# A decoder layer in float32 pairs: weight lows of the first FFN piece on VectorE, and TensorE's loop over the FFN pieces written out

## The reference

```
xm = rmsnorm(h, p['norm_mlp_g'])
h = h + jnp.square(jax.nn.relu(xm @ p['w_up'])) @ p['w_down']     # w_up 2048 x 8192, w_down 8192 x 2048
y = rmsnorm_final(h)
```

## Time and profile before

| | |
|---|---|
| median of 3 runs | 2808.96 us (2808.72 to 2814.73) |
| the profiled execution | 2811.47 us, of which the span of its instructions is 2809.4 us |
| TensorE busy | 2740.9 us, 98% of the span; mean granted clock 0.989 |
| VectorE, ScalarE, GpSimd busy | 55%, 32%, 22% |
| the first FFN piece on TensorE | 1359.0 to 1568.9 us |
| pieces 1 to 7 | 1568.9 us to the final transposes, some 174 us each |

### The profile page before, as it was taken

The page is one execution under the profiler, slowest core; times in us unless marked ns, Lnnn a source line. Parts: engine busy times, 40 slices in busy tenths (PEclk is TensorE's granted clock), DMA queues, the critical chain, the costliest instruction groups (busy, mean ns, idle before and its releaser), DMA issues.

```text
span 2809.4 us, 51396 instructions
## 1 busy us (share of the span) xinstructions
PE 2740.9 (98%) x21572; PEld 2624.0 (93%) x21572; DVE 1536.6 (55%) x2077; ACT 911.6 (32%) x1187; POOL 627.6 (22%) x278
## 2 busy tenths in 40 slices
PE   9999999999999999899988999999999999999998
PEld 7999998777999888699988999999999999999998
DVE  4677836667222344422354665746557465574765
ACT  5221125445222211232232332514325143251442
POOL 2455434675444322244330000000000000000000
PEclk9999999999999999999999999999999999999999
DMA  6733445655432655543227455464554635546443
GB/s 191 144 101 100 105 127 158 180 166 161 159 94 83 195 195 195 173 128 112 91 60 209 116 163 156 116 187 121 156 155 122 185 110 163 148 124 184 110 139 110
DMA packets 543266, 399.71 MB, mean 142 GB/s; under 512 B 35145, under 2 KB 464047, under 8 KB 541615
## 3 DMA queue, kind: packets, MB, share of 16 engines
q1 hardware_dynamic: 471032, 294.02, 36.4%
q10 hardware_dynamic: 72027, 102.69, 12.2%
HBM read 343.10 MB, written 53.84 MB: 141 GB/s over the span
## 4 chain that ended last, share of the span: by engine, by line
PE 72%; issue 13%; POOL 7%; DVE 5%; ACT 1%; DMA 1%; SPq 0%; POOLq 0%; DVEq 0%; ACTq 0%
PE lin L2248 26%; PE lin L1643 21%; PE aux L2213 17%; POOL wlo L883 4%; PE lin L2213 3%; POOL wlo L925 3%; PE aux L1920 1%; PE aux L1965 1%; DVE turn L2300 1%; PE lin L1733 0%; DVE rot L2300 0%; PE aux L1911 0%; PE aux L1810 0%; PE aux L1806 0%; DVE mixl L2300 0%
## 5 line engine op out<-in xcount | busy, mean ns | idle before, releaser
L883 POOL TENSOR_TENSOR wlo<-raw,whi 128x1024 fp32r<-128x1024 f32 x188 | 461.5, 2458 | 716.2 <-ACT whi L965 522.0
L2248 PE MATMUL lin<-fh,whi 128*128 128x260 f32 x2048 | 578.7, 283 | 13.0 <-DVE part L3127 10.4
L2248 PE MATMUL lin<-fl,whi 128*128 128x260 f32 x2048 | 578.9, 283 | 0.0
L2248 PE MATMUL lin<-fh,wlo 128*128 128x260 f32 x2048 | 578.9, 283 | 0.0
L2248 PEld LDWEIGHTS lin<-fh,whi 128*128 128x128 f32 x2048 | 387.0, 189 | 13.4 <-DVE wlo L3018 10.6
L1475 ACT ACTIVATE whi<-raw 128x1024 fp32r<-128x1024 f32 x212 | 224.2, 1058 | 511.8 <-DVE hr L3131 401.0
L2248 PEld LDWEIGHTS lin<-fh,wlo 128*128 128x128 f32 x2048 | 387.5, 189 | 0.0
L2248 PEld LDWEIGHTS lin<-fl,whi 128*128 128x128 f32 x2048 | 386.7, 189 | 0.0
L3018 DVE TENSOR_TENSOR wlo<-raw,whi 128x1024 fp32r<-128x1024 f32 x238 | 290.3, 1220 | 29.3 <-ACT whi L1475 29.3
L965 ACT ACTIVATE whi<-raw 128x1024 fp32r<-128x1024 f32 x140 | 147.5, 1058 | 472.6 <-PE lin L1643 324.0
L3127 DVE TENSOR_TENSOR part<-lin,rB 128x520 f32<-128x520 f32 x128 | 89.5, 699 | 382.4 <-PE lin L2248 375.9
(11 more groups left out here) (483 smaller groups left out, 6703.5 us busy)
## 6 DMA issues: line engine op xcount, KB each, us to landing
raw<-in_w_up SPq DMA_DIRECT2D x128, 512.0 KB, 4.3
raw<-in_w_down SPq DMA_DIRECT2D x128, 512.0 KB, 4.4
hr<-hscr ACTq DMA_DIRECT2D x128, 260.0 KB, 3.3
raw<-in_w_in SPq DMA_DIRECT2D x60, 512.0 KB, 3.9
hscr<-hr ACTq DMA_DIRECT2D x112, 260.0 KB, 2.1
raw<-in_w_out SPq DMA_DIRECT2D x32, 512.0 KB, 3.9
raw<-in_w_q SPq DMA_DIRECT2D x32, 512.0 KB, 4.0
piece<-in_cache_mem_k SPq DMA_DIRECT2D x32, 512.0 KB, 6.0
```

The source lines that it names most:

```text
L883: pool.tensor_tensor(wlo[:, slot, :], raw[:, slot % 2, :], whi[:, slot, :].bitcast(F32), ALU.subtract).then_inc(s.w_lo, 1)
L2248: mm = pe.matmul(lin[:, 2 * i + f, 0:HALF], w, x[:, kk, HALF * f:HALF * f + HALF], start=(first and m == 0 and part == 0), stop=(last and ...
```

## The change

It has two parts.

1. In the first FFN piece GpSimd makes no lows from the second pair on; its loop ends one turn after `T_MLP` begins, and the two units of `w_down` go too. VectorE makes them (`lo_slot`, `lo_down`). On VectorE and ScalarE the work of a pair is no longer in blocks: the four weight units, the two tiles and the two sets of sums are interleaved (`up_tile`, `up_low`, `sums_of`, `sums_low`).
2. On TensorE `with pe.Fori(1, N_CHUNK) as c` becomes `for c in range(1, N_CHUNK)`: the seven pieces stand one after the other in its list, with constants in the waits.

```diff
-            with pool.Fori(T_O + 1, T_MLP + QUADS) as T:
+            with pool.Fori(T_O + 1, T_MLP + 1) as T:
                 lo_turn(T)
-            for n in range(2):
-                pool.wait_ge(s.w_hi, unit_of(0, n) + 1)
-                pool.tensor_tensor(wlo[:, n, :], RAW4[n], whi[:, n, :].bitcast(F32), ALU.subtract).then_inc(s.w_lo, 1)
...
             for p in range(QUADS):
-                if p < QUADS - 1:
-                    hi_turn(p + T_MLP + 1)
-                else:
-                    hi_down(0, 0)
-                    hi_down(0, 1)
-                up_pair(p)
+                last = p == QUADS - 1
+                hi_down(0, 0) if last else hi_slots(p + T_MLP + 1, (0,))
                 combined(2 * p)
+                hi_down(0, 1) if last else hi_slots(p + T_MLP + 1, (1,))
+                up_tile(p, 0)
                 combined(2 * p + 1)
+                if not last:
+                    hi_slots(p + T_MLP + 1, (2, 3))
+                up_tile(p, 1)
...
-            with pe.Fori(1, N_CHUNK) as c:
+            for c in range(1, N_CHUNK):
                 for u in range(QUADS):
                     quad(c, u)
...
+            def lo_slot(T, slot):
+
+                n = 4 * T + slot
+                if n == 4 * (T_MLP + 1):
+                    v.wait_ge(s.w_lo, n)
+                v.wait_ge(s.w_hi, n + 1)
+                v.tensor_tensor(wlo[:, slot, :], raw[:, slot % 2, :], whi[:, slot, :].bitcast(F32),
+                                ALU.subtract).then_inc(s.w_lo, 1)
...
             for p in range(QUADS):
-                up_pair(p)
+                last = p == QUADS - 1
+                lo_down(0, 0) if last else lo_slot(T_MLP + p + 1, 0)
+                sums_of(2 * p)
+                up_tile(p, 0)
+                sums_low(2 * p)
+                lo_down(0, 1) if last else lo_slot(T_MLP + p + 1, 1)
+                up_low(p, 0)
+                sums_of(2 * p + 1)
+                if not last:
+                    lo_slot(T_MLP + p + 1, 2)
+                sums_low(2 * p + 1)
+                up_tile(p, 1)
                 if p == 0:
                     inverse(6, D, 2)
-                combined(2 * p)
-                combined(2 * p + 1)
+                if not last:
+                    lo_slot(T_MLP + p + 1, 3)
+                up_low(p, 1)
```

More of the change, by code:

```diff
@@ L1580, in down, with up_tile @@
                     square_h(n) if end else store_h(c, n)
[L1582 to L1587, removed]
+            def up_tile(p, i):
+                act.wait_ge(s.tile_free, 2 * p + (O_MLP + i + 1))
+                act.activation(hsqF[:], upr[:], ACT.Square).then_inc(s.up_sq, 1)
+                act.wait_ge(s.up_sq, 4 * p + 2 * i + 2)
+                act.activation(fh[:, 2 * p + i, :], hsqF[:], ACT.Copy).then_inc(s.hid_hi, 1)
             def combined(k):
@@ L2219, in quad @@
                 Q = quad_of(c, q)
-                if not (isinstance(c, int) and c == 1 and q == 0):
+                if Q > 0:
                     pe.wait_ge(s.up_sq, act_n(Q - 1, 4))
@@ L2989, in _, with up_tile, up_low, sums_of @@
                 step.leave(7)
[L2990 to L3002, removed]
+            def lo_slot(T, slot):
[5 more added lines that the diff above has]
+                                ALU.subtract).then_inc(s.w_lo, 1)
+            def up_tile(p, i):
+                v.wait_ge(s.pe_unit, 4 * (T_MLP + p) + 2 * i + 2)
+                if p == 0 and i == 1:
+                    v.wait_ge(s.stat_mm, stat_n(6))
+                if p + i > 0:
+                    v.wait_ge(s.hid_lo, 2 * p + i)
+                v.tensor_scalar(halves(upr[:]), lin_tile(i), 0.0, None, ALU.max).then_inc(s.tile_free, 1)
+            def up_low(p, i):
+                v.wait_ge(s.hid_hi, 2 * p + i + 1)
+                v.tensor_tensor(fl[:, 2 * p + i, :], hsqF[:], fh[:, 2 * p + i, :].bitcast(F32),
+                                ALU.subtract).then_inc(s.hid_lo, 1)
+            def sums_of(k):
                 for j in range(2):
@@ L3009, in combined, with sums_low @@
                 tt(tsum[:, 3, :], tsum[:, 1, :], msum[:, 1, 0, :], ALU.subtract, s.t_dve)
-                v.wait_ge(s.up_sq, 4 * (k // 2) + 2 + k % 2 + 1)
+            def sums_low(k):
+                v.wait_ge(s.up_sq, 2 * k + 1)
                 tt(tl[:, :, k, :], tsum[:], th[:, :, k, :].bitcast(F32), ALU.subtract, s.t_dve)
@@ L3015, in lo_unit @@
                 v.wait_ge(s.w_hi, n + 1)
-                if n == unit_of(0, 2):
-                    v.wait_ge(s.w_lo, n)
                 v.tensor_tensor(wlo[:, slot, :], src, whi[:, slot, :].bitcast(F32), ALU.subtract).then_inc(s.w_lo, 1)
```

## The result

The changed kernel takes 2775.8 us (median of 4 runs, 2773.1 to 2778.8) against 2809.8 us before (2808.7 to 2814.7): ratio 0.9876, 95% interval 0.9859 to 0.9893, 34.0 us less. The forecast was 2775.0 us, 34.0 us less.

A forecast was written before the change was run, and what follows sets the result against it. TensorE, busy 98% of the span, bounds the kernel, through its waits and low clock. First piece 25.6 plus loop 8.4 gives 34.0 us off 2811.5; against the median before, 2775.0 us forecast, range 2770 to 2787.

The forecast's parts named there:

- The first piece, 25.6 us: Second pair to end of first FFN piece: 17.8 us idle plus low clock behind it, 25.6 us in all, would go.
- cause (a): First piece: next pair's roundings stand behind both `th`, GpSimd's lows come late; waits of 2.0, 2.8 and 2.6 us would go.
- ScalarE's late roundings: First piece: ScalarE rounds the next pair's first two units only behind both `th`; the two roundings last 1.99 us.
- Cause (b): End of first piece: loads for `down` wait for the last `tl`, making `part` late; TensorE's 10.4 us wait would go.
- E - 1.5: First piece's last pair: the last `tl` would end near 1.5 us before the last `w_up` unit ends (E).
- The cover of 0.7 us at E: First `down`: `part` done at E + 10.8, TensorE supplied to E + 11.5; in time by 0.7 us, the thinnest cover.
- `fl`: VectorE's subtraction in the first piece: 0.70 us each time instead of up to 1.81, moving nothing in the sum.
- The loop, 8.4 us: TensorE's pieces 1 to 7 written out: 13.5 us of return costs leave, 5.1 come back as boundary waits; net 8.4 us.
- the momentary low clock: At one of the loop's six returns the clock falls for a moment: 10.41 against 8.87 us for the same 72 matmuls.
- the prediction's lower bound of 6.9: Loop's gain is 6.9 us if the momentary low clock belongs to chance and comes elsewhere.
- The seven waits: Piece boundaries after the change: seven waits of about 0.6 us for VectorE's low replace the 10.4 us "issue" entry.
- stay near 159: TensorE's instruction queue: its packet count would stay near 159 with the loop written out.

The follow-up runs named there:

- woven_gpsimd: Changed kernel (woven order, loop written out) with the first piece's 14 lows left on GpSimd; 2777.8 us, ratio to before 0.9887.
- block_vector: Kernel before with the loop written out and the first piece's 14 lows on VectorE, in the old block order; 2808.2 us, ratio 1.0000.
- loop_only: Kernel before with only TensorE's loop over pieces 1 to 7 written out, first piece as it was; 2804.1 us, ratio 0.9978.
- piece_only: Changed kernel with TensorE's loop over pieces 1 to 7 put back, so only the first piece is new; 2781.2 us, ratio to before 0.9895.
- loop_bodies: Changed kernel, VectorE's next-piece S1, S2 moved ahead of the last `part`, two TensorE loops before the FFN lengthened to 384 and 576 matmuls; 2768.1 us, single run.
- short_loops: Changed kernel with units 4 to 15 of `down` as a TensorE loop of 192-matmul bodies in all eight pieces; 2779.2 us, ratio to before 0.9902.

## Why the prediction was right

- *The first piece, 25.6 us.* Measured 25.5 from the mark to piece 1. That the old order is cause (a) holds: with the order woven the waits go even with the lows on GpSimd (woven_gpsimd), and with both engines in the old order they turn into waits for relus (block_vector). ScalarE's order was never changed without VectorE's, so how much of it is ScalarE's late roundings, as the prediction has it, is read from the trace and not tested. The order carried this part. The change's first half as its title has it, lows on another engine, did not. The prediction took both together and left that open.
- *Cause (b).* The load of unit 2 of the first `down` started at 1477.80 us before, behind the last `tl`. The last `tl` now ends at 1447.6, and the load starts with the end of the last `w_up` unit (E, 1449.3):

```profile
1449.34 0.37 SPq L825 DMA_DIRECT2D raw<-in_w_down  x1
```

That fits the prediction's step and its E - 1.5 for the last `tl`. No run took (b) away alone, so the split of the 25.5 us between (a) and (b) is only read from the waits before.
- *The cover of 0.7 us at E.* `part` of the first `down` unit starts when TensorE is through with it; ScalarE's rounding of unit 2 began 4.1 us behind E, not 5.6, as its load landed earlier:

```profile
1459.42 0.70 DVE L3136 TENSOR_TENSOR part<-lin,rB 128x520 f32<-128x520 f32 x1 [3.64 <-PE lin L2245]
```

That is E + 10.1, as worked out, with VectorE idle for 3.6 us ahead of it. The load's side had 1.5 us more cover than I gave it.
- *`fl`.* It takes 0.69 to 0.70 us each time, as foreseen, and that moved nothing, as woven_gpsimd shows. There the stretched ones end 0.55 us behind GpSimd's low, so that one engine waits for the other's whole instruction.
- *The loop, 8.4 us.* Measured 8.2 between the two profiles, 8.1 in loop_only, 7.0 between piece_only and the changed kernel. The difference is the momentary low clock, the prediction's lower bound of 6.9. The seven waits are 0.6 us each as at piece 1 before.
- *What I had wrong.* The packets of TensorE's instructions fell from 159 to 149 where I said they would stay near 159: each long return brought 1.7 packets more than its body has (12.9 against 11.25). No time shows for these ten packets by themselves.
- *Straight code and far branches.* No matmul of the straight code in loop_only waits for its instructions, and the branch of 3.5 us is gone with its idle time. The Trainium skill, "Runtime: NRT & Kernel Launch", section "Instruction fetch mechanics", has both, straight code mostly hidden and a stall at a target outside a window; the trace agrees. Its window of two 16 KiB pages does not fit TensorE here, and the measurement decides: the bodies of 384 and 576 matmuls are 3 and 4.5 packets of 16.4 KB long and returned in 0.21 to 0.24 us without being fetched again.
- *The median* came out at the forecast within 0.8 us, which is luck as to its last digits: the executions of before alone lie between 2801 and 2816 us, and the mark scatters by 8 us.
- *Not additive in the timed medians:* 5.5 and 28.4 us for the parts give 33.9, but each is uncertain by some 3 us; by the marks the parts give 8.1 + 26.7 = 34.8 against 33.7, and the momentary low clock (1.5 us, in the run of before alone) is in both.

## What to carry to other kernels

Where an engine that feeds TensorE works in blocks, replay its list against TensorE's deadlines one unit at a time; weaving the lists of both engines unit by unit took away 25 us here, while moving the work to a faster engine in the old order lost 6 us. A loop at run time on TensorE was free here up to a body of 576 matmuls and cost 2 to 4 us a return at 1440; and before writing it out, look at the one boundary that is entered without a branch, since it shows the wait that the stall has been hiding. Read small gains from a mark inside the profile and not from the whole span, when the part ahead scatters.

## What the runs showed of the hardware that I had not expected

- The cost of a return is a step: branch 0.21 to 0.24 us at bodies of 192, 384 and 576 matmuls, 3.3 to 3.9 us at 1440 and 2880. By the packets on TensorE's instruction queue the body is not fetched again up to 576 (157 packets in loop_bodies, 125 in short_loops) and is at each return at 1440 (159 in piece_only).
- Two-input instructions of VectorE beside GpSimd's subtractions can be stretched up to four times: `msum` 2.74 us for 0.70, `fl` 2.84 for 0.70. The stretched `fl` each ended 0.55 us behind the end of the subtraction beside them. Where `fl` began first (before, 1462.67 us) it took 0.70 and the subtraction 2.88 for 2.40.
- A return's idle time of 1.9 to 2.0 us was followed by 16 or 17 matmuls at half clock (some 3.5 us, of which 1.6 are lost) in 3 of 14 cases, and not in others as long.
